# Third stage of a two-block transformer step: side projection first, gate and q by token block

## What is computed

```
x = x + _moe(hn, ...)                                   # end of the experts: x2
gate = jax.nn.sigmoid(_rmsnorm(x, g_ple_norm[i]) @ w_ple_gate[i])   # 1024 x 1024
x = x + (p[i] @ w_ple_proj[i]) * gate                   # p: 256 x 256; x3
...
h = rms_norm(x, norm1_pre[i])                           # second block
proj = h @ w_in[i]                                      # q, k, v, z, xbc, dt, gates
```

## Time and profile before

| | |
|---|---|
| median of three runs | 1627.27 us (1626.36 to 1627.76) |
| the profiled execution's own time | 1627.78 us |
| its span, first to last instruction | 1626.0 us |
| mean granted TensorE clock | 0.983 |
| TensorE busy | 1481.1 us, 91% |
| VectorE, ScalarE, GpSimd busy | 467.8, 421.4, 459.9 us |
| chain that ended last | TensorE 53%, DMA 35%, VectorE 5%, ScalarE 3%, GpSimd 1% |

### The profile page before, as it was taken

One profiled execution on the slowest core, in us unless ns is written; L12 is line 12 of the kernel. 1 busy time (PEld: TensorE's weight loads), 2 busy tenths in 40 slices (PEclk: granted clock), 3 DMA queues, 4 the chain that ended last, 5 costly groups with the idle time before them and its releaser, 6 DMA issues.

```text
span 1626.0 us, 18685 instructions
## 1 busy us (share of the span) xinstructions
PE 1481.1 (91%) x7559; PEld 845.7 (52%) x7560; DVE 467.8 (29%) x806; ACT 421.4 (26%) x530; POOL 459.9 (28%) x356
## 2 busy tenths in 40 slices
PE   6998999998898989888988989888999998999998
PEld 5866633333333323333332333333798776789986
DVE  5526511211111111111111111112357187233311
ACT  5365310100101001001010010013645643353332
POOL 5924100000000000000000000003588573779994
PEclk9999899999999999999999999999999999999999
DMA  9531599999999999999999999999455322545540
GB/s 343 186 104 53 220 429 428 428 428 427 427 428 428 428 427 428 427 428 427 428 427 429 426 428 428 427 427 373 138 182 169 116 94 75 171 154 186 190 169 26
DMA packets 91172, 502.26 MB, mean 309 GB/s; under 512 B 7836, under 2 KB 38164, under 8 KB 66388
## 3 DMA queue, kind: packets, MB, share of 16 engines
q1 hardware_dynamic: 89600, 498.71, 76.0%
q10 hardware_dynamic: 1491, 2.36, 0.5%
HBM read 500.00 MB, written 1.05 MB: 308 GB/s over the span
## 4 chain that ended last, share of the span: by engine, by line
PE 53%; DMA 35%; DVE 5%; ACT 3%; issue 2%; POOL 1%; SPq 1%; ACTq 1%; DVEq 0%
DMA ring<-in_w_up_gate 35%; PE PS L854 13%; PE PS L520 10%; PE PS L521 9%; PE PS L522 9%; PE PS L872 4%; PE PS L823 1%; POOL w_low L2183 1%; DMA ring<-in_w_ple_gate 1%; PE PS L1107 1%; SPq L422 1%; ACT w_high L1228 1%; PE PS L861 0%; DVE arena L1862 0%; DVE arena L1865 0%
## 5 line engine op out<-in xcount | busy, mean ns | idle before, releaser
L2183 POOL TENSOR_TENSOR w_low<-ring,w_high 128x512 fp32r<-128x512 f32 (+1 forms) x352 | 459.7, 1341 | 1144.8 <-ACT w_high L1228 1143.9
L854 PE MATMUL PS<-ring,arena 128*64 128x512 f32 x2048 | 457.3, 598 | 35.2 <-DMA ring<-in_w_up_gate 35.2
L854 PEld LDWEIGHTS PS<-ring,arena 128*64 128x64 f32 x2048 | 141.7, 137 | 334.1 <-issue 266.3
L872 PE MATMUL PS<-ring,arena 128*64 128x512 f32 x1024 | 235.3, 613 | 28.0 <-ACT arena L1365 28.0
L1356 ACT ACTIVATE arena<-arena 128x512 f32<-128x512 f32 x32 | 20.1, 630 | 766.1 <-DVE arena L1859 766.1
L1228 ACT ACTIVATE w_high<-ring 128x2048 fp32r<-128x2048 f32 (+1 forms) x89 | 166.3, 1882 | 116.1 <-PE PS L522 101.3
L872 PEld LDWEIGHTS PS<-ring,arena 128*64 128x64 f32 x1024 | 75.1, 140 | 166.2 <-issue 166.2
L1859 DVE TENSOR_SCALAR arena<-PS 128x512 f32<-128x512 f32 x32 | 22.1, 692 | 467.0 <-PE PS L854 467.0
L520 PE MATMUL PS<-w_high,XNT_h 128*128 128x512 f32 (+1 forms) x336 | 135.7, 404 | 5.9 <-DVE XNT_l L1583 4.3
L520 PE MATMUL PS<-XNT_h,w_high 128*128 128x256 f32 (+1 forms) x464 | 132.0, 284 | 3.5 <-DVE XNT_l L1573 2.6
L521 PE MATMUL PS<-w_low,XNT_h 128*128 128x512 f32 (+1 forms) x336 | 132.5, 394 | 0.0
(11 more groups left out here) (357 smaller groups left out, 1447.7 us busy)
## 6 DMA issues: line engine op xcount, KB each, us to landing
ring<-in_w_up_gate SPq DMA_DIRECT2D x128, 2048.0 KB, 24.5
ring<-in_w_down SPq DMA_DIRECT2D x64, 2048.0 KB, 22.2
ring<-in_w_in SPq DMA_DIRECT2D x35, 1024.0 KB, 5.8
ring<-in_w_gate_up SPq DMA_DIRECT2D x22, 1024.0 KB, 5.2
ring<-in_w_down SPq DMA_DIRECT2D x11, 1024.0 KB, 4.8
ring<-in_w_out SPq DMA_DIRECT2D x8, 1024.0 KB, 5.0
ring<-in_w_ple_gate SPq DMA_DIRECT2D x4, 1024.0 KB, 22.3
ring<-in_w_ssd_proj SPq DMA_DIRECT2D x4, 1024.0 KB, 5.0
```

What stands on the lines that cost most here:

```text
L854: ins = nc.tensor.matmul(PS[64 * (n % 2):64 * (n % 2) + 64, 4 + n // 2, :], x, w[:, n * 512:(n + 1) * 512], start=False, stop=c == KC - 1, ...
L872: ins = nc.tensor.matmul(PS[64 * n:64 * n + 64, 7, :], lhs, w[:, k, n * 512:(n + 1) * 512], start=(j, k) == (0, 0), stop=(j, k) == (1, 3))
L2183: ins = nc.gpsimd.tensor_tensor(LOW[raw_slot(key)][:, at], slot(raw_slot(key))[:, at], HIGH[m % BUF][:, at].bitcast(F32), ALU.subtract)
```

## The change

- The piece of the side projection comes first behind the experts, ahead of the four gate pieces. The four pieces split in the branch are now it and three gate pieces; the last gate piece and the two of q come by `split_to`, behind the first norm.
- The four transposes of p stand between the expert loop and the branch, into bank 4. ScalarE copies them (`side_high`) between the second and the third split, VectorE subtracts (`low(PT[1], ...)`) ahead of its branch and of the addition of x2.
- TensorE makes the side projection of token block 0 into banks 6 and 7 ahead of the transposes of x2, that of token block 1 into banks 2 and 3 behind them.
- The gate goes by `pair_group`: per column group first token block 0, then 1. Both column groups of block 0 lie in banks 4 and 5, of block 1 in 0 and 1. `first_rows` counts block 0.
- The stage's end goes by token block: ScalarE does sigmoid, table load, square and root for one block and then for the other; VectorE multiplies, adds, scales. The first block's evacuation stands on ScalarE behind the second sigmoid and on VectorE behind the second multiplication.
- TensorE transposes block 0 of the norm, waits for both sigmoids, does q's 24 products of block 0, then transposes block 1 (`between`), then q's other 24.

The transposes, evacuations and banks are given by lists (`BLOCK_BANKS`) instead of a first bank; where the stages before and behind use these functions, their banks are the same as before. The helper `norm_block` of the last stage is moved ahead, its extra wait to its callers.

```diff
@@ -154,8 +154,8 @@
     ROUNDS = E + (PASSES - 1) * E
     base_c = before_experts + PER_EXPERT * ROUNDS
     late = len(pieces)
+    piece("ple_proj", a["w_ple_proj"][0], 2, D)
     column_groups("ple_gate", a["w_ple_gate"][0], 0, 2)
-    piece("ple_proj", a["w_ple_proj"][0], 2, D)
     column_groups("q", w_in2, 0, 1)
     piece("dt", w_in2[:, 3328:3360], KC, 32)
     for c in range(6):
@@ -388,7 +388,8 @@
         XBC_BANK = (2, 3, 4, 5, 6, 7)
         UNITS = [(q, c) for q in range(4) for c in range(2)]
         FILL = (0, 1, 2, 3)
-        NORM_BANK = (4, 4, 4, 4, 0, 0)
+        NORM_BANK = (4, 4, None, None, None, 0)
+        BLOCK_BANKS = {2: (4, 5, 0, 1), 3: (4, 5, 6, 7), 4: (0, 1, 2, 3)}
         FIRST_ROUNDS = (6, 4, 5, 7)
         LATE_IN = 7 * 16
         FIRST_LOW = 2
...
 
-            def pair_group(tag, g, lhs, bank_of, first_rows=False):
+            def pair_group(tag, g, lhs, bank_of, first_rows=False, between=None):
 
                 for tb in range(NTB):
+                    if tb == 1 and between:
+                        between()
                     for h in range(2):
...
@@ -927,8 +931,14 @@
                                                YS[64 * n:64 * n + 64, :], start=False, stop=False, skip_group_check=True)
                     ins.then_inc(sem("scattered"), 1)
 
+            for kc in range(2):
+                for tb in range(NTB):
+                    ins = nc.tensor.transpose(PS[:, 4, kc * 256 + tb * P:kc * 256 + (tb + 1) * P],
+                                              t3(PIN, 2)[:, tb, kc * P:(kc + 1) * P], ident)
+            ins.then_inc(sem("pT_ps"), 1)
             with pe.If(any_more > 0):
                 last_scatter()
+                pe.wait_ge(sem("pT"), 1)
                 with pe.Fori(0, PASSES - 1) as p:
                     with pe.Fori(0, E) as e:
                         more = pe.value_load(flag_i[0:1, bass.ds(p * E + e, 1)])
@@ -963,33 +973,30 @@
             pe.nop()
 
 
-            norm_T(2)
-            takes("xnT", 8, True)
-            for g in range(2):
-                for half in range(2):
-                    half_group("ple_gate", g, half, XNT, lambda tb: 2 * tb + g)
-                if g == 0:
-                    for kc in range(2):
-                        for tb in range(NTB):
-                            ins = nc.tensor.transpose(PS[:, 6, kc * 256 + tb * P:kc * 256 + (tb + 1) * P],
-                                                      t3(PIN, 2)[:, tb, kc * P:(kc + 1) * P], ident)
-                    ins.then_inc(sem("pT_ps"), 1)
+            def ple_proj(tb, bank):
+
+                w = split_view("ple_proj")
+                for n in range(2):
+                    for k in range(2):
+                        ins = product(PS[:, bank + n, :], [x[:, k * 256 + tb * P:k * 256 + (tb + 1) * P] for x in PT],
+                                      [x[:, k, n * 512:(n + 1) * 512] for x in w], start=k == 0, stop=k == 1)
+                return ins
+
             pe.wait_ge(sem("pT"), 1)
             arrived("ple_proj")
-            w = split_view("ple_proj")
-            for tb in range(NTB):
-                for n in range(2):
-                    for k in range(2):
-                        ins = product(PS[:, 4 + 2 * tb + n, :], [x[:, k * 256 + tb * P:k * 256 + (tb + 1) * P] for x in PT],
-                                      [x[:, k, n * 512:(n + 1) * 512] for x in w], start=k == 0, stop=k == 1)
-                if tb == 0:
-                    ins.then_inc(sem("first_rows"), 1)
-            ins.then_inc(sem("w_used"), 1)
-
-
-            norm_T(3)
+            ple_proj(0, 6)
+            norm_T(2)
+            ple_proj(1, 2).then_inc(sem("w_used"), 1)
+            takes("xnT", 8, True)
+            pair_group("ple_gate", 0, XNT, lambda tb: (4, 0)[tb])
+            pair_group("ple_gate", 1, XNT, lambda tb: (5, 1)[tb], first_rows=True)
+
+
+            block_transposes(XN, BLOCK_BANKS[3], "xnT_ps", "xn", 6, (0,))
             takes("xnT", 12, True)
-            pair_group("q", 0, XNT, lambda tb: tb)
+            pe.wait_ge(sem("ple_gate"), 2)
+            pair_group("q", 0, XNT, lambda tb: tb,
+                       between=lambda: block_transposes(XN, BLOCK_BANKS[3], "xnT_ps", "xn", 6, (1,)))
 
             narrow_rows("dt", 7)
...
@@ -1363,7 +1370,13 @@
                 nc.scalar.activation(SPT, PS[:, 7, 0:256], ACT.Copy).then_inc(sem("sT_slots"), 1)
                 act.wait_ge(sem("hT_ps"), e + 1)
                 nc.scalar.activation(HTS, PS[:, 6, :], ACT.Copy).then_inc(sem("hT"), 1)
+            def side_high():
+
+                act.wait_ge(sem("pT_ps"), 1)
+                nc.scalar.activation(PT[0], PS[:, 4, :], ACT.Copy).then_inc(sem("pT_high"), 1)
+
             with act.If(any_more > 0):
+                side_high()
                 with act.Fori(0, PASSES - 1) as p:
                     with act.Fori(0, E) as e:
                         more = act.value_load(flag_i[0:1, bass.ds(p * E + e, 1)])
@@ -1391,24 +1404,30 @@
 
                     act.wait_ge(sem("w_used"), before_experts + PER_EXPERT * (E - 1) + EXPERT_SLOT.index((RAW + m % BUF) // 2 * 2) + 1)
                     split(m)
+                    if m == late + 1:
+                        side_high()
             done_splits[0] = late + BUF
             act.nop()
 
             load_table(ACT.Sqrt)
             block_evac(2, V_PLE)
             norm(2, "x2")
-            split_to(number[("ple_proj")])
-            act.wait_ge(sem("pT_ps"), 1)
-            nc.scalar.activation(PT[0], PS[:, 6, :], ACT.Copy).then_inc(sem("pT_high"), 1)
-            split_to(number[("ple_gate", 1, 1)] + 3)
-            act.wait_ge(sem("w_used"), place[("ple_gate", 1, 1)] + 1)
+            split_to(number[("ple_gate", 1, 1)] + 2)
             for tb in range(NTB):
+                load_table(ACT.Sigmoid)
                 act.wait_ge(sem("xn"), 2 * 2 + tb + 1)
-                nc.scalar.activation(SG[:, tb * D:(tb + 1) * D], banks(2 * tb, 2), ACT.Sigmoid,
+                if tb == 0:
+                    act.wait_ge(sem("first_rows"), 2)
+                else:
+                    act.wait_ge(sem("w_used"), place[("ple_gate", 1, 1)] + 1)
+                nc.scalar.activation(SG[:, tb * D:(tb + 1) * D], banks((4, 0)[tb], 2), ACT.Sigmoid,
                                      scale=stat[:, 6 + tb:7 + tb]).then_inc(sem("ple_gate"), 1)
-            split_to(number["ple_proj"] + 3)
-            norm(3, "x3")
-            block_evac(3, V_N1)
+                if tb == 1:
+                    block_evac(3, V_N1, (0,))
+                load_table(ACT.Sqrt)
+                square(tb, "x3")
+            split_to(number["dt"])
+            block_evac(3, V_N1, (1,))
             act.dma_start(ROTT, a["consts"][:, C_ROT:C_ROT + 2 * T]).then_inc(sem("late_in"), 16)
             silus = iter(range(CC))
...
+            def norm_block(i, tb, src=X, dst=XN):
+
+                dve.wait_ge(sem("rms"), 2 * i + tb + 1)
+                link(V.reciprocal(stat[:, 6 + tb:7 + tb], stat[:, 2 + tb:3 + tb]))
+                ts(dst[:, tb * D:(tb + 1) * D], src[:, tb * D:(tb + 1) * D], stat[:, 6 + tb:7 + tb], None, ALU.mult).then_inc(sem("xn"), 1)
...
@@ -1870,6 +1893,8 @@
                     group_round_out(XG[(u // GROUP + 1) % 2], q)
             count[0] = start + 2 * E
             start = count[0]
+            dve.wait_ge(sem("pT_high"), 1)
+            low(PT[1], PS[:, 4, :], PT[0]).then_inc(sem("pT"), 1)
             with dve.If(any_more > 0):
                 with dve.Fori(0, PASSES - 1) as p:
                     with dve.Fori(0, E) as e:
@@ -1917,17 +1942,17 @@
             for tb in range(NTB):
                 dve.wait_ge(sem("rms"), 2 * 2 + tb + 1)
                 V.reciprocal(stat[:, 6 + tb:7 + tb], stat[:, 2 + tb:3 + tb]).then_inc(sem("xn"), 1)
-            dve.wait_ge(sem("pT_high"), 1)
-            low(PT[1], PS[:, 6, :], PT[0]).then_inc(sem("pT"), 1)
-            for tb, (name, n) in enumerate((("first_rows", 2), ("w_used", place["ple_proj"] + 1))):
+            dve.wait_ge(sem("w_used"), place["ple_proj"] + 1)
+            for tb in range(NTB):
                 dve.wait_ge(sem("ple_gate"), tb + 1)
-                dve.wait_ge(sem(name), n)
                 x, sg = X[:, tb * D:(tb + 1) * D], SG[:, tb * D:(tb + 1) * D]
-                link(tt(sg, sg, banks(4 + 2 * tb, 2), ALU.mult))
+                link(tt(sg, sg, banks((6, 2)[tb], 2), ALU.mult))
+                if tb == 1:
+                    block_evac(3, V_N1, (0,))
                 tt(x, x, sg, ALU.add).then_inc(sem("x3"), 1)
-            dve.wait_ge(sem("x3"), 2)
-            norm(3)
-            block_evac(3, V_N1)
+                dve.wait_ge(sem("x3"), tb + 1)
+                norm_block(3, tb)
+            block_evac(3, V_N1, (1,))
 
 
```

More of the change, by code:

```diff
@@ L1575, in norm_evac, with block_evac @@
                     ins.then_inc(sem("xnT"), 1)
-            def block_evac(i, gain):
-                for tb in range(NTB):
```

(2 more changed lines are left out.)

39 lines of the change are left out of this document (17 added, 22 removed).

## The result

| | before | after |
|---|---|---|
| median | 1627.43 us (22 runs, 1626.33 to 1629.21) | 1629.86 us (22 runs, 1627.76 to 1636.80) |
| profiled execution, its span | 1627.78, 1626.0 us | 1630.72, 1628.9 us |
| mean granted TensorE clock | 0.983 | 0.981 |

The ratio after to before is 1.0015 (1.0010 to 1.0021): slower by 2.4 us. That is clear of zero, though within the 0.2% that the prediction called no change, and 0.26 us above the end of its range. The prediction had 1626.1.

The account below looks back on a forecast made before the run. TensorE, 91% busy, was taken as the bound. The gate ends 3.8 us earlier, the tail grows from 19.0 to 21.65, so q ends 1.1 earlier: 1626.1 us against a median of 1627.27; range 1622.4 to 1629.6.

Parts of the forecast that it names:

- the first block's chain: Behind the gate's first block: sigmoid to scaling runs under the second block's products; transposes start 0.75 us after the gate's end.
- the clock term of the tail: Around q: low-clock stretches behind the two breaks cost 1.65 us and 0.8 us.
- The head: Expert loop to gate: side products fill the wait before the gate, which ends at 1163.9 instead of 1167.7, 3.8 us gained.
- From transposes to q: Behind the gate: added table load and second sigmoid delay q, which starts 4.8 us after the gate's end, after 3.0 idle.
- The rival that a switch costs more than its load: ScalarE before the second sigmoid: running empty adds 1.28 us, so q ends 0.2 later than before, 1627.5 us; chance 0.06.
- The second break: Between q's two blocks: second transposes and their evacuation take 3.1 us, 2.1 of it idle on TensorE.
- The hidden second scaling: Beside q's first block: the second block is scaled 9.4 us after the gate's end, before TensorE comes at 10.4 or later.
- The faster rival (clock stays high): Loop's last addition and both parts of q run at 2.4 GHz: q ends 4.9 us earlier, 1622.4 us; chance 0.24.
- the slower rival, low clock outlasting the head: Low clock through all TensorE work before the gate: q ends 4.6 us later than before, 1631.9 us; chance 0.10.

Follow-up runs that it names:

- a_head: The change's head (side projection first, gate by token block) with the stage's end put back as in the kernel before; 1628.18 us, 1.0002 of before.
- b_psum: The change, with the product of gate and side projection written back to PSUM and added from there; 1627.85 us, 1.0000 of the kernel before.
- r_after: The change again, unchanged, for a second trace; 1629.24 us in one run.
- g_busy2: The change with 6 and 4 dummy TensorE products filling the two breaks around q; 1627.45 us in one run.
- r_before2: The kernel before, unchanged, traced once more to see the scatter of the expert loop's end; 1628.84 us in one run.
- c_early: The change, with the second block's transposes between the halves of q's first block, 12 products earlier; 1626.06 us, 0.9993 of the kernel before.
- e_best: The change with the addition from PSUM, the second block's transposes 12 products earlier and 6 dummy products ahead of q; 1626.24 us, 0.9989 of before.

## Why the prediction was wrong

Two steps failed: the first block's chain, in which the addition was taken at 1.23 us and took 2.18 beside GpSimd, and the clock term of the tail, taken at 2.45 us and measured at 3.65. By its own steps, for the profiled execution. The prediction had q's end at 1185.6, it came at 1189.37, 3.8 later; behind q the program takes what it took (439.53 for 439.47). Counted from the loop's end, where its scatter is out, the prediction had 57.9, and the two traces of the change have 60.70 and 61.37: 2.8 and 3.4 more.

- **The loop's end**: 1.06 later, scatter, no step of the prediction.
- **The head** held. The last addition came later by nearly what was said (+0.6, with 0.4 put in), nothing waited before the gate, and no weight came late. The low stretch fell on the addition (3.53) and not on the side products, at about the same cost. The gate's start shifted by 4.05 against the loop's end, where 3.85 was said: 0.2. The gain stood, but in a_head, where the tail is as before, little of it is left: the side products had been the cover of the first block's chain (2.0 of break more), and the low stretch behind the longer break was twice as long.
- **The first block's chain** is the step that failed first: "multiply 1.22 and add 1.23 to G-1.8 ... Its transposes start at G+0.75, nearly without a break". Measured G+2.0 (gate's end 1165.17, transposes 1167.17). Of the 1.25, 0.96 is the addition, priced from the earlier trace rows, where GpSimd was idle, though the prediction itself had placed q's low parts "near 1157 and 1162", beside that addition. b_psum shows the cause. The other 0.3 is made of handoffs of 0.04 to 0.11 between the chain's instructions, which the sum took too short.
- **From transposes to q**: 4.05 said, 4.12 measured, the second sigmoid and the added table load included. The rival that a switch costs more than its load is out. The drain of about 1380 ns that the Trainium skill, "ScalarE: Activation LUTs", section "What ACT_TABLE_LOAD costs", adds to the load is not seen in this trace: the load starts 0.31 behind the root's start, and the sigmoid 1.53 behind the load's.
- **The clock** is the second step that was mis-sized: 1.65 + 0.8 taken, 2.1 + 1.55 measured. The first stretch was of double length, which no row at that place had shown. The earlier trace rows had one elsewhere: its window of 6 us lies inside a stretch of 6.8, from 186.2 to 193.0. The second was put half way between the rows of 1.70 and 1.92, and a break of 2.05 brought it whole in three traces of three (the change, r_after, b_psum); with the break filled in g_busy2 it stayed away. The length of a break was a weak guide to begin with: in the same trace of before a break of 1.28, shorter than the 1.70 that brought nothing, ended at 178.96, and a low stretch began at 179.2.
- **The second break**: 2.1 said, 2.05 measured. The hidden second scaling was ready at 1175.92, hidden as said.

1.06 + 0.2 + 1.25 + 0.1 + 0.5 + 0.8 make 3.9 for the 3.8. Two small slips stand in the prediction's sums and move nothing: 4.8 + 5.6 + 3.1 + 5.6 make 19.1, not 19.2, and 1186.7 takes in the whole duration of q's last product, where the distance between starts, by which the new end is summed, gives 1186.53. The faster rival (clock stays high) did not occur in the change; for q it is what g_busy2 forced. Of the slower rival, low clock outlasting the head, the change's traces show nothing, but a trace of the kernel before does (r_before2, below): there 6.8 us of it fell ahead of the gate, and the gate started when it always did.

The miss was avoidable. The trace of before had the slow addition, in the first block; VectorE and GpSimd there:

```profile
155.25 1.23 DVE L1735 TENSOR_TENSOR arena<-arena 128x1024 f32<-128x1024 f32 x1
156.51 2.19 DVE L1736 TENSOR_TENSOR arena<-arena 128x1024 f32<-128x1024 f32 x1
...
155.56 2.06 POOL L2183 TENSOR_TENSOR w_low<-ring,w_high 128x512 fp32r<-128x512 f32 x1 [6.03 <-ACT w_high L1228]
```

The first addition started ahead of GpSimd's and took 1.23, and GpSimd's took 2.06 where one of eight takes 1.26 in the change; the second started behind it and took 2.19. Whichever started second took longer.

## What to carry over

Price a moved instruction from a row that has the same neighbours on the other engines, and ask which cover the moved work gave to what stayed. If two engines meet in the same stretch, look for the same operation elsewhere in the trace beside the same partner before its duration is taken. Where a chain is cut in two, put the second transposes as far ahead as their operand allows; the break between them costs its length and, here, also the clock of the products behind it.

## What the runs showed of the hardware

- A VectorE addition with both operands in SBUF took 2.18 us beside GpSimd's subtraction and 1.22 without, and 1.22 beside it with one operand in PSUM. From the slow addition's start to GpSimd's end by the trace it was 1.09, a little more than the 0.96 lost. The Trainium skill, "SBUF — State Buffer", section "Who interferes with whom", says that a VectorE instruction with two SBUF inputs contends with a GpSimd instruction that reads SBUF, and that whoever comes second stands still until the first has ended; the traces agree, within that 0.13.
- A low stretch can last twice the 3.4 us of the earlier trace rows, also with TensorE mostly busy: 6.8 in the change, and in r_before2, a trace of the kernel before, 6.8 too (this window at 0.56), under the addition and the transposes of x2.

```profile
1132.00:1139.80 7.80, 6.71 (x24) 0.56 0.86 312
```

- Whether a low stretch comes behind the loop's exit varies with the run: the same head had one in eight of ten traces and none in c_early and e_best, and the gate then started 12.5 instead of 14.1 us behind the gathers. What decides it stays open, and so does what decides between 3.4 and 6.8.
- The break at TensorE's branch behind the loop was 2.5 to 3.0 us in all traces and stood behind the work queued ahead of it. Which part of loop exit and branch makes it was not tried.
